# Second attention: both heads' scores made as a pair, low passes in the two halves of the array

## What is computed

```python
def forgetting_attention(q, k, v, cum_logf):     # (B, S, 8, 64)
    s = jnp.einsum('bqhd,bkhd->bhqk', qb, k).astype(jnp.float32) * scale
    s = s + Fb[..., :, None] - Ft[:, :, None, :]
    s = jnp.where(mask[None, None], s, -jnp.inf)
    p = jax.nn.softmax(s, axis=-1).astype(v.dtype)
    return jnp.einsum('bhqk,bkhd->bqhd', p, v)
...
def indexer_sparse_attention(q, k, v, q_idx, k_idx, w_idx, rel_bias):
    _, sel = lax.top_k(iscore, topk)
    logits = jnp.einsum('bqhd,bqkhd->bhqk', qb, kg).astype(jnp.float32) * scale
    logits = logits + jnp.transpose(bias, (0, 3, 1, 2))
    p = jax.nn.softmax(logits, axis=-1).astype(vg.dtype)
    return jnp.einsum('bhqk,bqkhd->bqhd', p, vg)
```

## Time and profile before

| | us |
|---|---|
| median of three runs | 1345.73 |
| lowest, highest | 1345.5, 1347.48 |
| profiled execution | 1345.89 |
| its span, first to last instruction | 1344.1 |
| TensorE matmuls busy | 1335.3 (99%) |
| weight loads busy | 1093.7 (81%) |
| VectorE busy | 764.2 (57%) |
| ScalarE busy | 526.7 (39%) |
| GpSimd busy | 562.6 (42%) |
| mean granted TensorE clock | 0.999 |

### The profile page before, as it was taken

One profiled execution on the slowest core, in us unless ns is written; L12 is line 12 of the kernel. 1 busy time (PEld: TensorE's weight loads), 2 busy tenths in 40 slices (PEclk: granted clock), 3 DMA queues, 4 the chain that ended last, 5 costly groups with the idle time before them and its releaser, 6 DMA issues.

```text
span 1344.1 us, 18070 instructions
## 1 busy us (share of the span) xinstructions
PE 1335.3 (99%) x6378; PEld 1093.7 (81%) x6378; DVE 764.2 (57%) x1097; ACT 526.7 (39%) x831; POOL 562.6 (42%) x230
## 2 busy tenths in 40 slices
PE   9999999999999999999999999999999999999998
PEld 8888888888888888777877777888878888888886
DVE  4555678575664655877788774443562241432365
ACT  6344234422423224254466665322355133242333
POOL 5333444554553635525222224444435534345351
PEclk9999999999999999999999999999999999999999
DMA  7223245656655645423322323334423423324231
GB/s 231 80 85 91 89 139 167 175 169 175 193 168 161 186 142 166 111 92 97 63 78 64 95 70 89 110 94 111 126 77 99 120 82 108 92 85 117 79 94 63
DMA packets 212807, 155.74 MB, mean 116 GB/s; under 512 B 8932, under 2 KB 193760, under 8 KB 212744
## 3 DMA queue, kind: packets, MB, share of 16 engines
q1 hardware_dynamic: 212280, 154.43, 40.0%
q10 hardware_dynamic: 464, 0.48, 0.1%
HBM read 152.75 MB, written 4.74 MB: 117 GB/s over the span
## 4 chain that ended last, share of the span: by engine, by line
PE 98%; DVE 1%; ACT 0%; issue 0%; DVEq 0%; POOL 0%; ACTq 0%; POOLq 0%
PE ps L589 67%; PE ps L1144 11%; PE ps L1025 3%; PE ps L1088 3%; PE ps L735 2%; PE ps L991 1%; PE ps L1004 1%; PE ps L1174 1%; PE ps L977 1%; PE ps L978 1%; PE ps L964 0%; PE ps L981 0%; PE ps L652 0%; PE ps L647 0%; PE ps L938 0%
## 5 line engine op out<-in xcount | busy, mean ns | idle before, releaser
L550 POOL TENSOR_TENSOR w_lo<-raw,w_hi 128x1024 fp32r<-128x1024 f32 x222 | 559.6, 2528 | 751.1 <-ACT w_hi L1230 731.1
L589 PE MATMUL ps<-u_hi,w_hi 128*128 128x512 f32 x944 | 377.0, 399 | 0.2 <-issue 0.2
L589 PE MATMUL ps<-u_hi,w_lo 128*128 128x512 f32 x944 | 368.6, 390 | 0.0
L589 PE MATMUL ps<-u_lo,w_hi 128*128 128x512 f32 x944 | 367.9, 390 | 0.0
L1230 ACT ACTIVATE w_hi<-raw 128x1024 fp32r<-128x1024 f32 x222 | 232.1, 1054 | 289.5 <-PE ps L589 113.0
L589 PEld LDWEIGHTS ps<-u_hi,w_lo 128*128 128x128 f32 x944 | 177.3, 188 | 37.5
L589 PEld LDWEIGHTS ps<-u_hi,w_hi 128*128 128x128 f32 x944 | 178.3, 189 | 34.7 <-issue 0.8
L589 PEld LDWEIGHTS ps<-u_lo,w_hi 128*128 128x128 f32 x944 | 177.7, 188 | 34.2
L589 PE MATMUL ps<-y_hi,w_hi 128*128 128x512 f32 x320 | 124.9, 390 | 0.0
L589 PE MATMUL ps<-y_hi,w_lo 128*128 128x512 f32 x320 | 124.6, 389 | 0.0
L589 PE MATMUL ps<-y_lo,w_hi 128*128 128x512 f32 x320 | 124.6, 389 | 0.0
(11 more groups left out here) (330 smaller groups left out, 1884.5 us busy)
## 6 DMA issues: line engine op xcount, KB each, us to landing
raw<-w_in SPq DMA_DIRECT2D x69, 512.0 KB, 3.8
raw<-w_mlp SPq DMA_DIRECT2D x64, 512.0 KB, 4.0
adaw<-w_ada SPq DMA_DIRECT2D x32, 768.0 KB, 4.5
raw<-w_up SPq DMA_DIRECT2D x32, 512.0 KB, 6.7
raw<-w_down SPq DMA_DIRECT2D x32, 512.0 KB, 6.0
raw<-w_out SPq DMA_DIRECT2D x16, 512.0 KB, 4.5
bias_rows<-bias_rows SPq DMA_DIRECT2D x4, 635.0 KB
xtok<-x SPq DMA_DIRECT2D x4, 512.0 KB, 7.0
```

The costliest lines, as they stand in the source:

```text
L550: pool.tensor_tensor(w_lo[:, s, :], raw[:, s, :], w_hi[:, s, :], ALU.subtract).then_inc(lo_ready[s], 1)
L589: last = pe.matmul(ps[0:cols, bank, :], w[:, s, c], r[:, k, :], start=(k == ks[0] and w is w_hi and r is r_hi), stop=(k == ks[-1] and w is ...
```

## The change

- TensorE: `s_step` for one head becomes `s_pair` for both. It is called at even steps only, for scores n + 4 and n + 5, and issues both high passes, both low passes, the wait for the selection mask, and both masks.
- The low passes use 64 rows each: `half` is rows 0 to 63 for head 0 and 64 to 127 for head 1, of `q_dn` and of `k_both`.
- Scores go round three banks, SA, SB and 2, by score number, in place of one bank for each head. `logits` reads the same one. In the first group the second pair waits for bank 2, which the values used.
- The pair waits for the logits of score n - 2 alone. At the start of the first group the two pairs take the places of four score steps, and as many pieces are issued.
- VectorE no longer clears the other halves of `q_dn`, and the counts of `q_ready` are one lower.
- The number of matmuls stays the same: six for a pair.

```diff
--- before.py
+++ after.py
@@ -52,6 +52,7 @@
 
 SA, SB, TR, OU = 4, 5, 6, 7
 TURNS = (TR, 3)
+SCORES = (SA, SB, 2)
 LOOK = 4
 KEYROW = (NT - 1) * P
 TURNED = (NT - 1) * KEYROW + NT * P
@@ -965,23 +966,31 @@
                           ki[b:b + HD, 0:(i + 1) * P], start=True, stop=True).then_inc(sem("idx_s"), 1)
 
 
-            def s_step(p, n):
-                i, hh = n // 2, n % 2
-                if n == 0:
-                    pe.wait_ge(sem("q_ready"), 2 * p + 3)
+            def s_pair(p, i):
+
+                if i == 0:
+                    pe.wait_ge(sem("q_ready"), 2 * p + 2)
                     pe.wait_ge(sem("k_ready"), 2 * p + 2)
-                wait(pe, sem("att_logit"), 8 * p + n - 1)
-                keys = (i + 1) * P
-                bank, at = SA + hh, 2 * (p % 2) + hh
-                q = slice(i * P, (i + 1) * P)
-                pe.matmul(ps[:, bank, 0:keys], q_up[:, at, q], k_both[:, at, 0:keys], start=True, stop=False)
-                pe.matmul(ps[:, bank, 0:keys], q_dn[:, at, q], k_both[:, at, 0:keys], start=False, stop=False)
+                if p == 0 and i == 1:
+                    pe.wait_ge(bank_free[2], st_val.turn(2, 2))
+                n = 8 * p + 2 * i
+                wait(pe, sem("att_logit"), n - 1)
+                keys, q = (i + 1) * P, slice(i * P, (i + 1) * P)
+                banks = [SCORES[(n + hh) % 3] for hh in range(2)]
+                for hh, bank in enumerate(banks):
+                    at = 2 * (p % 2) + hh
+                    pe.matmul(ps[:, bank, 0:keys], q_up[:, at, q], k_both[:, at, 0:keys], start=True, stop=False)
+                for hh, bank in enumerate(banks):
+                    at, half = 2 * (p % 2) + hh, slice(hh * HD, (hh + 1) * HD)
+                    pe.matmul(ps[:, bank, 0:keys], q_dn[half, at, q], k_both[half, at, 0:keys], start=False, stop=False)
                 if p >= NQ:
                     pe.wait_ge(sem("sel_ready"), i + 1)
-                    last = pe.matmul(ps[:, bank, 0:keys], identb[:], sel[:, i, 0:keys], start=False, stop=True)
-                else:
-                    last = pe.matmul(ps[:, bank, keys - P:keys], identb[:], causalb[:], start=False, stop=True)
-                last.then_inc(sem("att_s"), 1)
+                for bank in banks:
+                    if p >= NQ:
+                        last = pe.matmul(ps[:, bank, 0:keys], identb[:], sel[:, i, 0:keys], start=False, stop=True)
+                    else:
+                        last = pe.matmul(ps[:, bank, keys - P:keys], identb[:], causalb[:], start=False, stop=True)
+                    last.then_inc(sem("att_s"), 1)
 
             def t_step(p, n):
                 i, hh = n // 2, n % 2
@@ -1060,9 +1069,10 @@
             pieces += [f for m in range(2) for s in range(2) for f in pairs(st_bra, s, m)]
             for _ in range(KC + LOOK - 2):
                 pieces.pop(0)()
-            for n in range(LOOK):
+            for i in range(LOOK // 2):
                 pieces.pop(0)()
-                s_step(0, n)
+                s_pair(0, i)
+                pieces.pop(0)()
             for p in range(2 * NQ):
                 for n in range(8):
                     if n == 1 and p > 0:
@@ -1073,8 +1083,8 @@
                         pv(p, 1)
                     t_step(p, n)
                     coming = 8 * p + n + LOOK
-                    if coming < 16 * NQ:
-                        s_step(coming // 8, coming % 8)
+                    if n % 2 == 0 and coming < 16 * NQ:
+                        s_pair(coming // 8, coming % 8 // 2)
                     pieces.pop(0)()
 
             def branch(m):
@@ -2280,8 +2290,6 @@
             dve.wait_ge(sem("masks"), 3)
             dve.tensor_copy(sel[:, 0, 0:P], causalb[:]).then_inc(sem("sel_ready"), 1)
 
-            dve.memset(q_dn[HD:P, 0:4:2, :].bitcast(F32), 0.0)
-            dve.memset(q_dn[0:HD, 1:4:2, :].bitcast(F32), 0.0).then_inc(sem("q_ready"), 1)
             dve.wait_ge(sem("fw_ready"), 1)
             dve.wait_ge(sem("norm_u"), before("n3") + KC)
             f = fw[0:HEADS, :]
@@ -2366,7 +2374,7 @@
                 else:
                     tab = tab2[:, 2 * (p % 2) + n % 2, T - keys:T]
 
-                dve.tensor_tensor_reduce(prob(n), ps[:, SA + n % 2, 0:keys],
+                dve.tensor_tensor_reduce(prob(n), ps[:, SCORES[(8 * p + n) % 3], 0:keys],
                                          tab, -(HD ** -0.5), -MASKED, ALU.add, ALU.min,
                                          mneg[:, n:n + 1]).then_inc(sem("att_logit"), 1)
 
@@ -2395,7 +2403,7 @@
                                   ).then_inc(sem("q_ready"), 1)
                 dve.tensor_tensor(q_dn[HD:P, at + 1, :], ps[HD:P, 0, :], q_up[HD:P, at + 1, :], ALU.subtract
                                   ).then_inc(sem("q_ready"), 1)
-                dve.wait_ge(sem("q_ready"), 2 * g + 3)
+                dve.wait_ge(sem("q_ready"), 2 * g + 2)
                 dve.sem_inc(bank_free[0], 1)
 
             def k_lows(g):
```

## The result

| | before | after |
|---|---|---|
| median, us (20 runs each, same chip) | 1345.45 | 1347.97 |
| lowest, highest | 1344.78, 1347.5 | 1347.38, 1350.98 |
| span of the profiled execution | 1344.1 | 1346.3 |
| TensorE matmuls busy | 1335.3 | 1337.1 |
| VectorE, ScalarE, GpSimd busy | 764.2, 526.7, 562.6 | 763.0, 527.1, 562.8 |

A forecast was written before the change was run, and what follows sets the result against it. The prediction took TensorE to bound the kernel: +2.6 us of its time in the second attention, less 1.1 us of absorbed waits, gave +1.5 us on 1345.73, so 1347.2 us. The range was 1344.8 to 1349.9 us.

The forecast's parts named there:

- TensorE bounds the kernel, and the second attention alone changes.: Whole kernel: 98% of the chain is TensorE, so only its instruction stream between 665 and 831 us counts.
- The price of an excursion: Entering and leaving half-array tiles on TensorE: drain, uncovered weight load, drain, 0.31 us for each of 32 pairs.
- Low and mask terms: Score pairs of the second attention: +0.23 us a causal group, +0.43 a selection group, +2.6 us of TensorE time.
- Rival 1: Low passes: no drains or loads drawn ahead, 1339.7 us, chance 0.10; entry load alone drawn ahead, 1344.8 us, chance 0.06.
- Rival 2: Low passes of a pair run one after the other, adding 4.4 us: 1351.6 us, chance 0.06.
- Rival 3: Next group's key lows come late because score 6 does; up to 0.6 us in six groups, 1350.8 us, chance 0.10.
- Of these 1.6 us I take 1.1 as absorbed: TensorE's waits in the first and fifth groups: slower TensorE arrives later and waits 1.1 us less, bounds 0 and 1.6.
- Nothing on the path: VectorE before the first indexer scores: two clears of 64x1024 go away, with no effect on the critical path.
- The total: Whole kernel: +2.6 us of TensorE time less 1.1 absorbed gives +1.5 us, 1347.2 us.

The follow-up runs named there:

- the two kernels with the hold: GpSimd's split of the query weights waits until VectorE has scaled block 1, added to the change (1346.72 us) and to the kernel before (1344.51 us).
- The experiment on full rows: The change with its low passes over all 128 rows and the clears of `q_dn` put back: 1344.5 us, ratio 0.9991 to the kernel before.
- a second couple: The change with both low passes of each pair issued twice inside one stay in the half-array tiles: 1351.45 us, ratio 1.0039 to before.
- all three kernels: GpSimd's query-weight split held until VectorE has scaled block 1: kernel before 1344.51, the change 1346.72, the change with full-row low passes 1342.77 us.
- the four kernels: The change 1347.97 us; the change with low passes issued twice 1351.45, with low passes first 1350.02, with GpSimd's split held back 1346.72.
- the five others: Kernel before 1345.45 us, with half-array low passes alone 1361.18, with GpSimd held back 1344.51; the change with full-row low passes 1344.5, plus GpSimd held back 1342.77.

## Why the prediction was right, and where it was not

- **TensorE bounds the kernel, and the second attention alone changes.** Right: 98% of the chain, and the region grew by 2.59 us where the median grew by 2.52.
- **The price of an excursion, 0.31 us from the earlier trace rows.** Right: 0.33 in the pair of the last group. Between full and half rows under the same order the causal group differs by 0.43 us, the selection group by 0.46, 3.6 us for 32 pairs: the excursions, less the streaming that they save.
- **Low and mask terms.** Right within 0.02 us at each width; both ends of each term were read at the same kind of row in the trace of before. The sum was +2.6; the table gives 2.4, the region less its waits (180.41 - 1.66 against 177.82 - 1.73) 2.66, and the two kernels with the hold 2.6.
- **Rival 1, no drains or loads drawn ahead.** Fell: 0.37 and 0.24 us of idle time before the loads. The experiment on full rows shows loads without that idle time. (Its sum had a slip: its pairs give -0.63 for a selection group and not -0.67, so about 1339.9.) What the Trainium skill says of contraction over 64 rows, "TensorEngine Tiling (Array Packing)", section Theoretical Speedup, held for the streaming (both passes in one row of 0.49 us) and not for the pair, since up to 0.21 us saved stands against 0.33 paid.
- **Rival 2, low passes one after the other.** Fell: 3 ns between their starts, and a second couple costs about one load or one streaming.
- **Rival 3, late keys.** Fell as it was put: no group waits because score 6 comes later. But its wait, on just those keys, did come in one group of six, with another cause.
- **"Of these 1.6 us I take 1.1 as absorbed": this is the step that failed.** The fifth group's wait did vanish, as forecast (0.64 to 0.69 us), and the first group's fell from 1.04 to 0.79. Yet a new wait of 0.87 us came in the third, so TensorE's waits in the region went from 1.73 to 1.66 us and nothing was absorbed on balance. The step took VectorE's chain as fixed ("which doesn't move with TensorE inside a group") and its waits as a stock that a slower TensorE can only use up. The earlier trace rows showed the fifth group's length, and the scaling of 2.56 us behind it was in VectorE's timeline of before; read beside the 0.62 of its neighbours it would have said that the wait hangs on who starts first, and that 0.2 us can make one such collision. In the fifth group of the change the collision is still there (2.72 us), but TensorE's step 1 comes 0.40 us behind the start of the scaling (752.29, 751.89) where before it came 0.67 ahead of it (750.23, 750.90), and doesn't meet it.
- **"Nothing on the path", of VectorE's clears.** No cost of the clears themselves shows. But VectorE's idle time of 0.24 us in the third group comes in just those kernels that leave them out, and so does the collision there, where GpSimd isn't held back. The waits that did go (0.64 and 0.25 us, 0.9 of the forecast 1.1) were made up for by the 0.87 behind that collision.
- **The total.** +1.5 forecast, +2.5 measured: +2.6 of TensorE and 0.1 absorbed on balance, instead of +2.6 and -1.1. It stays within the bounds given for absorption (0 to 1.6), which is why the range held.

That the collision sets the waits is shown by the two holds. That leaving out the clears brings the 0.24 us of idle time is shown only by which kernels have it: the change with the clears put back and nothing else was not run, and why two instructions fewer should put idle time there stays open.

## What to carry to other kernels

Two half-array matmuls between full-array ones pay a fixed price for going in and out, here about 0.33 us; count it against the streaming saved (here at most 0.21 us), and make the stay longer or leave it out. Put the load that leaves such tiles in the same place as a load that would be late anyway. Before you credit a slower engine with waits that it will cover, look for instructions of one kind with two durations: here their long form was a collision, and 0.2 us made a new one. One semaphore that put the other engine behind them took the long form away in all three kernels, at the price of one new wait of 0.8 us in one of them.

## What the runs showed of the hardware that was not expected

- Two scalings of 128x256 took 0.62 us or 2.56 to 2.73, depending on whether the second started 0.07 us ahead of GpSimd's subtraction or behind it (by 0.14 us in the third group of the change).
- VectorE stood idle for 0.24 us at one and the same instruction in the four kernels whose VectorE program is two instructions shorter, with GpSimd beside it or not, and didn't in the five others.
- A bf16 weight load behind fp32r matmuls, or an fp32r load across a change of tile shape, came late in the rows shown, behind passes 512 columns wide (0.24 to 0.37 us idle), while an fp32r load behind an fp32r pass on the same rows had no idle time (passes 0.23 us apart). The two causes of lateness do not add when they fall on one load, and cost 0.10 to 0.11 us more when they fall on two.
- Going from one half of the array to the other costs next to nothing: four low passes of 384 keys lie in 0.61 us, and the second two of them added 0.18 us where streaming them takes 0.17.
